# Dropping the two-unit lead of the softmax normalisation in three attention stages, and splitting a weight slab one unit earlier

## The reference

```python
# first network, layer 1: banded, with a sink and 256 context keys (called "window" below)
p = jax.nn.softmax(jnp.concatenate([s_win, s_ctx, sinks], axis=-1), axis=-1).astype(vb.dtype)
o = (jnp.einsum('bhgqk,bkhd->bqhgd', p[..., :kw], vb)
     + jnp.einsum('bhgqc,bchd->bqhgd', p[..., kw:kw + C], vc))
...
# second network: 8 + 8 heads with a relative bias ("ab"), then compressed, selected and
# windowed attention with gates ("nsa")
s = jnp.where(mask, s.astype(F32), -jnp.inf)
m = jnp.max(s, axis=-1, keepdims=True)
e = jnp.exp(s - m)
p = e / jnp.where(l > 0, l, 1.0)      # l is the sum of e
```

## Time and profile before

| | |
|---|---|
| median of 3 runs | 2886.06 us (2884.16 to 2892.09) |
| profiled execution, its own time | 2892.09 us |
| its span on the core | 2890.0 us |
| busy: PE, DVE, ACT, POOL | 2691.5, 1567.8, 1319.5, 22.0 us |
| window attention, first scores to first output projection | about 1667 to 1761 us of the span |
| ab attention | about 2061 to 2138 us |
| nsa attention | about 2538 to 2634 us |

### The profile page before, as it was taken

One profiled execution on the slowest core, in us unless ns is written; L12 is line 12 of the kernel. 1 busy time (PEld: TensorE's weight loads), 2 busy tenths in 40 slices (PEclk: granted clock), 3 DMA queues, 4 the chain that ended last, 5 costly groups with the idle time before them and its releaser, 6 DMA issues.

```text
span 2890.0 us, 40595 instructions
## 1 busy us (share of the span) xinstructions
PE 2691.5 (93%) x15609; PEld 2269.4 (79%) x15609; DVE 1567.8 (54%) x2288; ACT 1319.5 (46%) x2003; POOL 22.0 (1%) x35
## 2 busy tenths in 40 slices
PE   6999998998899999899999788998999998789998
PEld 4788786876688877688877657998779997768998
DVE  7444434885644432644323565555866567456655
ACT  6444323464544422544322354544456555345644
POOL 0000000000000000000000000000000001000000
PEclk9999998999999999999999889999999999679999
DMA  6444542201344432344322301545325454302544
GB/s 245 174 160 161 189 144 73 94 23 44 117 173 147 169 106 102 117 169 150 131 93 96 117 1 61 187 160 194 116 86 186 165 190 159 107 1 74 189 175 146
DMA packets 52720, 374.81 MB, mean 130 GB/s; under 512 B 5822, under 2 KB 7034, under 8 KB 8736
## 3 DMA queue, kind: packets, MB, share of 16 engines
q1 hardware_dynamic: 50288, 360.73, 34.7%
q0 software_dynamic: 1920, 12.27, 1.3%
q10 hardware_dynamic: 432, 0.73, 0.1%
HBM read 372.55 MB, written 7.39 MB: 131 GB/s over the span
## 4 chain that ended last, share of the span: by engine, by line
PE 84%; DVE 9%; ACT 4%; issue 3%; DMA 1%; SPq 0%; DVEq 0%; ACTq 0%
PE acc L1632 25%; PE acc L1633 24%; PE acc L1634 24%; PE bank L1703 4%; DVE sc L1538 1%; DVE prod L543 1%; ACT sc L1027 1%; DVE wlo L1112 1%; DVE rs L1139 1%; DMA ada_raw<-in_slabs 1%; PE acc L2025 1%; PE bank L1738 1%; ACT whi L669 1%; DVE hlo L1200 1%; PE bank L1993 1%
## 5 line engine op out<-in xcount | busy, mean ns | idle before, releaser
L1112 DVE TENSOR_TENSOR wlo<-raw,whi 128x1024 fp32r<-128x1024 f32 x666 | 799.4, 1223 | 822.7 <-ACT whi L669 821.9
L669 ACT ACTIVATE whi<-raw 128x1024 fp32r<-128x1024 f32 x666 | 684.5, 1053 | 866.3 <-PE acc L1634 773.2
L1632 PE MATMUL acc<-hhi,whi 128*128 128x256 f32 (+1 forms) x2800 | 941.5, 336 | 51.9 <-DVE hlo L1200 35.9
L1633 PE MATMUL acc<-hlo,whi 128*128 128x256 f32 (+1 forms) x2800 | 936.7, 335 | 0.0
L1634 PE MATMUL acc<-hhi,wlo 128*128 128x256 f32 (+1 forms) x2800 | 935.8, 334 | 0.0
L1632 PEld LDWEIGHTS acc<-hhi,whi 128*128 128x128 f32 x2800 | 539.4, 193 | 113.4 <-issue 59.9
L1634 PEld LDWEIGHTS acc<-hhi,wlo 128*128 128x128 f32 x2800 | 539.3, 193 | 50.7
L1633 PEld LDWEIGHTS acc<-hlo,whi 128*128 128x128 f32 x2800 | 539.5, 193 | 49.0 <-issue 0.2
L1632 PE MATMUL acc<-ghi,whi 128*128 128x512 f32 (+1 forms) x1056 | 363.1, 344 | 22.5 <-DVE glo L1268 15.1
L1633 PE MATMUL acc<-glo,whi 128*128 128x512 f32 (+1 forms) x1056 | 361.5, 342 | 0.0
L1634 PE MATMUL acc<-ghi,wlo 128*128 128x512 f32 (+1 forms) x1056 | 361.4, 342 | 0.0
(11 more groups left out here) (263 smaller groups left out, 2577.4 us busy)
## 6 DMA issues: line engine op xcount, KB each, us to landing
raw<-in_slabs SPq DMA_DIRECT2D x333, 1024.0 KB, 4.8
ada_raw<-in_slabs SPq DMA_DIRECT2D x8, 1024.0 KB, 22.5
skew_dram<-lines_dram POOLq DMA_DIRECT2D x1, 6144.0 KB, 24.0
bt<-skew_dram POOLq DMA_DIRECT2D x4, 1024.0 KB, 7.6
x<-in_x_in SPq DMA_DIRECT2D x1, 2048.0 KB, 17.9
out<-x SPq DMA_DIRECT2D x1, 1024.0 KB, 4.8
rope<-in_rope POOLq DMA_DIRECT2D x1, 512.0 KB, 3.8
mask<-in_mask POOLq DMA_DIRECT2D x1, 512.0 KB, 4.6
```

Of the source, the lines that this page charges most:

```text
L669: nc.scalar.activation(whi[:, n % 2, cols], raw_of(n, cols), ACT.Copy).then_inc(ready, 1)
L1112: nc.vector.tensor_tensor(wlo[:, n % 2, cols], raw_of(n, cols), whi[:, n % 2, cols].bitcast(F32), ALU.subtract).then_inc(low, 1)
L1632: nc.tensor.matmul(out, w[0], xx[0], start=first, stop=False)
L1633: nc.tensor.matmul(out, w[0], xx[1], start=False, stop=False)
```

## The change

The constant AHEAD is dropped. DVE no longer runs `normalised` for units 0 and 1 ahead of its loop, and body u runs `normalised(u)` instead of `normalised(u + 2)`. `biased` stays three units ahead. Nothing moves on PE, ACT, POOL or SP. In the ab stage the first half of each slab split `lo` moves from bodies 4, 12, 20, 28 to bodies 3, 11, 19, 27; the second half stays in bodies 6, 14, 22, 30.

```diff
-AHEAD = 2
...
                 for u in range(LEAD):
                     biased(u)
-                for u in range(AHEAD):
+                for u in range(UNITS):
                     normalised(u)
-                for u in range(UNITS):
-                    if u + AHEAD < UNITS:
-                        normalised(u + AHEAD)
                     if u + LEAD < UNITS:
                         biased(u + LEAD)
...
-                    if st.what == "ab" and u % 8 in (4, 6):
+                    if st.what == "ab" and u % 8 in (3, 6):
                         lo(st.n0 + u // 8 + 2, halves=(u % 8 // 6,))
```

## The result

The changed kernel took 2909.88 us (median of 4 runs, 2903.15 to 2910.61) against 2886.31 for the one before: ratio 1.0074, 95% interval 1.0052 to 1.0094. The medians differ by 24 us, the ratio gives 21. The forecast was 2885.0, range 2877 to 2894. It was slower by more than 0.3%, to which I had given 0.12.

A forecast was written before the change was run, and what follows sets the result against it. PE, busy 2691.5 of 2890.0 us, was taken as the bound, so only its waits or clock matter. nsa -8.7, window -2.0 and ab +9.6 gave -1.1 us; forecast 2885.0 us, no change, range 2877 to 2894 for 8 in 10.

The forecast's parts named there:

- Gains in nsa and window: DVE no longer waits for ACT's latest exponential in nsa, 8.7 us; PE's waits at the window's end shrink, 2.0 us.
- ab's stalls: In ab, DVE's extras exceeding PE's cover stall PE before the next transpose, 13.3 us together.
- The last, forecast at 2.4: Body 30 of ab: `lo`, ahead of `normalised(31)`, waits for ACT's copy; PE stalls 2.4 us before the last transpose.
- Net 9.6: Loss in ab: stalls of 13.3 us, against today's waits of 2.8 and 0.9 us.
- the 13.3 in the list: Sum in us of PE's stalls in ab, listed body by body from 3 to 30.
- The 0.15 us of signalling: Allowance in DVE's chain from scores to transpose: some 0.15 us in nsa, 0.16 in ab.
- it falls as today, at the end and for as long: Clock in ab: at its lower level only from about 2134 to 2144, as today, so no change.
- The term for the clock in ab: Assumed no change; bounds: not falling gives back up to 5 us, one more mid-stage fall costs up to 8.
- The price of a fall: One 21 us stretch at half speed, as at nsa's beginning, costs 10.5 us less about 2.5 of covered stalls: 8.
- the slower rival: Clock falls mid-ab after body 3 or 11: once, 2893 us, chance 0.08; more than once, 2901 us, 0.06.
- no wait inside ab exceeded 0.9 us: Reading of the trace before the change: the clock fell in ab after waits none of which exceeded 0.9 us.
- the two finished rows: The transposes' reserve under the lead of two, which absorbs DVE's extras in ab today; the change removes it.

The follow-up runs named there:

- experiment 1: Lead dropped in window and nsa only, ab as in the kernel before; 2873.4 us, ratio 0.9958 to the kernel before.
- experiment 4: Kernel before with only `lo` moved to bodies 3, 11, 19, 27, lead of two kept; 2916.1 us, ratio 1.0073 to the kernel before.
- experiment 6: Experiment 4 plus ten dense unread matmuls on PE in body 8 of ab; 2888.1 us, ratio 1.0004 to the kernel before.
- experiment 7: Changed kernel plus one burst of 30 dense unread matmuls on PE in body 16 of ab; 2905.1 us.
- experiment 5: Changed kernel with PE's waits in ab filled by dense unread matmuls; 2885.9 us, ratio 0.999 to the kernel before.
- experiment 9: Changed kernel with a lead of one in all three stages, `lo` in bodies 4 and 6; 2870.6 us, ratio 0.9939 to the kernel before.
- experiment 2: The change in ab only, window and nsa as in the kernel before; 2927.0 us, ratio 1.0141 to the kernel before.
- experiment 3: Changed kernel with first `lo` halves put back in bodies 4, 12, 20, 28; 2907.7 us, ratio 1.0063 to the kernel before.
- experiment 8: Changed kernel with a lead of one in ab, none elsewhere, `lo` in bodies 4 and 6; 2871.1 us, ratio 0.9946 to the kernel before.

## Why the prediction was wrong

- **Gains in nsa and window: right.** 8.7 and 2.0 forecast, 9.0 and 2.3 in the two traces; 12 us for the whole kernel in experiment 1. How long nsa's beginning stays at the lower clock moves both sides alike: with about 15 us of it nsa took 93.6 us with the lead of two (experiments 4 and 6) and 82.6 to 84.5 without it or with one; with about 23 us, 95.3 and 96.5 against 87.5 to 88.4.
- **ab's stalls: right, but for the last.** Each of the six before the fall within 0.1 us. Of the later ones experiment 7 shows 0.45, 0.57, 0.34 and 1.04 us behind bodies 19, 22, 26 and 27, forecast at 0.4, 0.5, 0.3 and 1.2. The last, forecast at 2.4, was 1.51 there and 1.40 in the changed kernel. Net 9.6 forecast, 9.4 with the clock held (experiment 5), some 0.8 of it from the last fillings. Against the 74.0 us of ab in experiment 9, which hardly waits, that is 12.4, for the 13.3 in the list. The 0.15 us of signalling in each chain is what PE took behind ACT's copy in the kernel before (0.15 ahead of the transposes at 2104.57); behind DVE's row it took 0.05 in the changed kernel.
- **The step that failed: "I assume that it falls as today, at the end and for as long, which changes nothing."** The clock fell in the middle of ab in every profiled execution that had its unfilled stalls (the changed kernel and experiments 2, 3 and 7), and in experiment 4 with a single one of 1.25 us. The term for the clock in ab, put at nothing, measured 20.6 us in the changed kernel (ab 107.0 against the 86.4 of experiment 5).
- **The price of a fall was wrong too.** I took the 21 us at the start of nsa for the length of one stretch, "8 us". They are only the end of one: the clock had been down since 2475, for some 62 us before nsa began, and it came back under nsa's own matmuls, 15 to 24 us into the stage in every profile of this case:

```profile
2476.00:2537.00 61.00, 40.80 (x201) 39.06 (x201) 22.54 (x43) 19.28 (x32) 2.82 (x5) 0.50 0.22 75
2538.00:2559.00 21.00, 19.50 (x71) 13.84 (x70) 11.98 (x68) 8.84 (x34) 0.00 (x0) 0.50 0.00 0
2561.00:2628.00 67.00, 59.14 (x377) 43.45 (x376) 40.58 (x224) 35.62 (x129) 0.00 (x0) 1.00 0.00 1
```

  Under ab's matmuls, once it had fallen in the stage's middle, the clock did not come back as long as scores stood among them: without a burst such a fall lasted about 68, 78, 72 and 99 us in the changed kernel and experiments 3, 4 and 2, into the projection or, in experiment 4, to the last value matmuls. Against the ab of experiments 5 and 6, where the clock held, it was worth 20.6 us in the changed kernel, 28.6 in experiment 4 and 27.7 in experiment 2. I had the mechanism as the slower rival, with its place (behind body 3 or 11, so ahead of the transposes of 4 or 12; it was there in three of the four profiles with unfilled stalls, and ahead of those of 10 in experiment 3), and gave it 0.14 in two parts because nsa held its clock, 1.00 from 2561 to 2628 above, in spite of waits every other unit. ab did not.
- **The waits ahead of a fall.** In the middle of ab the clock fell behind waits of 1.02 us (experiment 3), 1.25 (experiment 4), 1.63 (the changed kernel), 2.15 (experiment 2) and 2.24 (experiment 7). It then stayed down for 48 us, up to the burst, in experiment 7, and for 68 to 99 us in the others; by itself it came back only at the stage's end, in experiments 1, 4 and 7. I gave such a fall too little weight. I also wrote that no wait inside ab exceeded 0.9 us before the fall of the kernel before; there is one of 1.59 us at 2063, 70 us ahead of that fall.
- **The reserve's worth.** I read the two finished rows as a cover against DVE's extras. Experiment 4 shows that even with both rows in reserve the wait of one engine further on, 1.25 us for the values' copy, was enough.

What stays open: what exactly of ab's mix of matmuls kept the clock down (busy for 69.00 of 69 us in experiment 4) when it came back under nsa's within 24 us, and why a given stall pulled it down in one execution and not in the next (the one in body 4 did in experiments 2 and 7, with 2.15 and 2.24 us, and with 2.15 us did not in the changed kernel). That the fall follows the stalls is shown by experiments 5 and 6, which fill them, and by 8 and 9, which remove them and add nothing; where in the stage it comes was not controlled.

## What to carry to other kernels

Price a stall on TensorE twice: its own length, and what it does to the clock of everything behind it until the clock comes back, here with the dense matmuls of the next stage. In ab, a stage of small matmuls, one wait of 1.25 us was worth 28 us (experiments 4 and 6). Read the price from the stage itself: under nsa's matmuls the clock came back 15 to 24 us into the stage, under ab's it stayed down for 68 to 99. A lead in a software pipeline is chosen between two costs: too long, and an engine asks for a result that it has only just ordered (lead two, nsa: 29.8 us of DVE's waits); too short, and the extras in that engine's queue reach TensorE (no lead, ab: six stalls of 0.2 to 2.2 us before the fall). Before dropping a lead for all stages, try the value in between.

## What the hardware showed that I had not expected

- PE was busy for 69.00 of 69 us and stayed at half clock, 0.50, all that time (experiment 4), while a burst of 5.6 us of 128x256 matmuls with 128 rows ended it (experiment 7).
- Adding 104 matmuls whose result nobody reads made the changed kernel 24 us faster (2909.9 to 2885.9).
- In experiments 3 and 4 the executions of one program fell into two groups, with nothing in between, and their mean clock parts them: 2889.6 and 2889.7 us at 0.951 against 2906 to 2912 at 0.941 to 0.943 in experiment 3, 2891 and 2895 at 0.953 and 0.951 against 2916 to 2918 at 0.942 to 0.944 in experiment 4.
